# Sliding mixer of a hybrid layer: value products of both head sets joined, query tiles in turn, queries laid out by halves

## What is computed

```python
proj = rms_norm(h, norm_mix) @ w_in        # [qA|kA|vA|qB|kB|vB]
oa = sliding_window_sink_attention(qa, ka, va, sinks, bias_a)   # 8 heads of 64, 2 key heads
ob = differential_attention(qb, kb, vb, lam, ...)               # 4 heads, dense, causal by chunk
h = h + concat(oa, ob) @ w_out

# sliding window: chunks of 64 queries, each sees its own chunk and the one before
sc = einsum('bcqhgd,bckhd->bchgqk', qc, kb) * HEAD_DIM ** -0.5 + bias
probs = softmax(concat([sc, sink]))[..., :-1]
o = einsum('bchgqk,bckhd->bcqhgd', probs, vb)
```

## Time and profile before

| | before |
|---|---|
| median of 3 runs (lowest, highest) | 1290.88 us (1290.87, 1291.49) |
| the profiled execution: its time, its span | 1291.0 us, 1289.2 us |
| granted TensorE clock, mean | 0.987 |
| PE busy | 94% of the span |
| VectorE, ScalarE, GpSimd busy | 68%, 40%, 25% |

### The profile page before, as it was taken

The page is one execution under the profiler, slowest core; times in us unless marked ns, Lnnn a source line. Parts: engine busy times, 40 slices in busy tenths (PEclk is TensorE's granted clock), DMA queues, the critical chain, the costliest instruction groups (busy, mean ns, idle before and its releaser), DMA issues.

```text
span 1289.2 us, 16975 instructions
## 1 busy us (share of the span) xinstructions
PE 1217.1 (94%) x6103; PEld 996.7 (77%) x6103; DVE 876.3 (68%) x1466; ACT 519.7 (40%) x1042; POOL 325.1 (25%) x335
## 2 busy tenths in 40 slices
PE   4999999999686799999999999999999999999997
PEld 3997787787565687888888888888888768888885
DVE  3432776777776276877877777878678997863442
ACT  4321664665554133433333333333344334642321
POOL 0000000444454011333223233133126780000000
PEclk9999999999889899999999999999999999999999
DMA  6364233012912411333323333323397534620101
GB/s 202 77 99 87 50 83 83 30 42 74 264 51 49 148 49 66 90 99 109 96 82 123 101 103 99 99 89 116 138 321 272 164 104 137 196 81 25 41 33 49
DMA packets 128669, 136.08 MB, mean 106 GB/s; under 512 B 15570, under 2 KB 93130, under 8 KB 128522
## 3 DMA queue, kind: packets, MB, share of 16 engines
q1 hardware_dynamic: 128586, 135.00, 34.9%
HBM read 96.77 MB, written 37.22 MB: 104 GB/s over the span
## 4 chain that ended last, share of the span: by engine, by line
PE 57%; DVE 7%; issue 2%; DMA 1%; SPq 0%; ACT 0%; POOL 0%; POOLq 0%; DVEq 0%; ACTq 0%
PE ps L1680 56%; DVE wbuf L1180 4%; DVE more L1180 1%; DVE h L1606 1%; PE ps L1690 1%; DMA raw<-u_ops 1%; DMA raw<-in_w_out 1%; PE ps L1886 1%; SPq L479 0%; ACT wbuf L799 0%; DVE conv L1403 0%; PE ps L2040 0%; POOL stat L678 0%; DVE xs L1465 0%; DVE gel L1673 0%
## 5 line engine op out<-in xcount | busy, mean ns | idle before, releaser
L1680 PE MATMUL ps<-act_t,wbuf 128*128 128x512 f32 x1200 | 288.8, 396 | 2.9 <-DVE wbuf L1180 2.9
L1680 PEld LDWEIGHTS ps<-act_t,wbuf 128*128 128x128 f32 x1200 | 225.7, 188 | 57.5 <-issue 3.3
L1680 PE MATMUL ps<-wbuf 128*128 128x512 f32 x912 | 217.1, 392 | 2.1 <-DVE wbuf L1180 2.1
L1680 PEld LDWEIGHTS ps<-wbuf 128*128 128x128 f32 x912 | 170.1, 188 | 40.9 <-DVE wbuf L1180 4.1
L1680 PE MATMUL ps<-act_t,wq 128*128 128x512 f32 x624 | 155.7, 402 | 3.6 <-DVE wq L1182 2.8
L1680 PEld LDWEIGHTS ps<-act_t,wq 128*128 128x128 f32 x624 | 114.6, 188 | 33.4 <-issue 7.4
L1180 DVE TENSOR_TENSOR wbuf<-raw,wbuf 128x512 fp32r<-128x512 f32 (+1 forms) x107 | 105.1, 983 | 21.3 <-ACT wbuf L799 21.0
L678 POOL TENSOR_TENSOR stat<-stat 128x1 f32<-128x1 f32 x32 | 17.6, 551 | 360.6 <-DVE stat L1189 360.6
L799 ACT ACTIVATE wbuf<-raw 128x512 fp32r<-128x512 f32 (+1 forms) x107 | 69.3, 649 | 93.3 <-PE ps L1680 65.5
L1680 PE MATMUL ps<-hx,wbuf 128*128 128x512 f32 x408 | 96.2, 391 | 0.0
L1680 PEld LDWEIGHTS ps<-hx,wbuf 128*128 128x128 f32 x408 | 76.5, 188 | 16.6
(11 more groups left out here) (197 smaller groups left out, 2056.8 us busy)
## 6 DMA issues: line engine op xcount, KB each, us to landing
u_ops<-wbuf_f SPq DMA_DIRECT2D x77, 256.0 KB, 2.2
raw<-u_ops SPq DMA_DIRECT2D x77, 256.0 KB, 2.7
raw<-in_w_ffn_in SPq DMA_DIRECT2D x33, 512.0 KB, 3.9
g_ffn<-in_w_ffn_in SPq DMA_DIRECT2D x11, 512.0 KB, 4.1
act_f<-in_w_ffn_out SPq DMA_DIRECT2D x21, 256.0 KB, 3.8
w_raw<-in_w_in SPq DMA_DIRECT2D x10, 512.0 KB, 4.5
wbuf_f<-in_w_ffn_out SPq DMA_DIRECT2D x18, 256.0 KB, 6.9
x_in<-in_x SPq DMA_DIRECT2D x8, 512.0 KB, 3.7
```

What stands on the lines that cost most here:

```text
L1680: return nc.tensor.matmul(dst, lhs, rhs, start=start, stop=stop)
```

## The change

It does four things. (1) Items run in another order: n is the tile of queries n // 2 and the head set n % 2. (2) The value products of both sets of a tile are joined in 12 matmuls of 256 columns, in every even round from 4 on; the turned probabilities alternate between two halves of `a_t`, the loop has a round more, `a_ohi` and `a_olo` belong to item n-4, and `mst_a` moves to a part of `e_t`'s room, in two pieces. (3) The queries lie by halves of the tokens; eight units come ahead of the loop, with the second head set's first half among them (`UNITS` puts unit 8 before unit 7), 16 half units in the loop, in rounds 0 to 3 and 6 to 17. (4) Loads of weight tiles move by one: tiles 3 to 6 are asked for ahead of the stores, then tile 7 + n // 4 after the store of item n = 0, 4, 8, 12.

```diff
@@ buffers
-    mst_a = a_t[:, :, HALF:2 * HALF]
+    mst_a = e_r[:, :, :, 2 * P:HALF]
-    q_a = wq[:, 4 * D:12 * D].rearrange("p (s l c u q) -> p s l c u q", s=2, l=2, c=NCH, u=2)
+    q_a = wq[:, 4 * D:12 * D].rearrange("p (h s l c u q) -> p h s l c u q", h=2, s=2, l=2, c=NCH // 2,
+                                          u=2)
@@ schedule
-    FIRST_UNITS = 7
+    FIRST_UNITS = 8
+    UNITS = [0, 1, 2, 3, 4, 5, 6, 8, 7, 9] + list(range(10, NUNIT))
+    def a_cols(n):
+        return slice(HALF * (n % 2), HALF * (n % 2 + 1))
+    def a_src(n):
+        return ps[0:HD, 6:8, 2 * P * (n % 2):2 * P * (n % 2 + 1)]
     def a_fill(n):
-        return n if n < NA + 2 else None
+        if n < 4:
+            return n
+        return n - 2 if 6 <= n < NA + 2 else None
@@ sync
-        for j in range(3, 6):
+        for j in range(3, 7):
             load_w(j)
         for n in range(NA):
             sp.wait_ge(S.a_olo, n + 1)
-            sp.dma_start(mix_a[n], bits(mst_a[0:HD])).then_inc(S.a_stored, 16)
+            sp.dma_start(mix_a[n % 2 * NT + n // 2].rearrange("d l (g x) -> d l g x", g=2), bits(mst_a[0:HD])
+                         ).then_inc(S.a_stored, 16)
             if n % 4 == 0:
-                load_w(6 + n // 4)
-            if n == NA - 1:
-                load_w(10)
+                load_w(7 + n // 4)
@@ scalar
...
         def after_unit(u):
-            if u % 2 == 1 and next_w[0] < NTILE:
+            if (u == FIRST_UNITS or u % 2 == 1) and next_w[0] < NTILE:
                 split_w(next_w[0])
...
+            if n == 2:
+                act.wait_ge(S.a_stored, 16 * NA)
-        for n in range(NA + 3):
+        for n in range(NA + 4):
-            if n >= 3:
-                m = n - 3
-                act.wait_ge(S.a_pv, m + 1)
+            if n >= 4:
+                m = n - 4
+                act.wait_ge(S.a_pv, m // 2 + 1)
                 if m >= 1:
                     act.wait_ge(S.a_stored, 16 * m)
-                copy(mst_a[0:HD, 0, :], ps[0:HD, 6 + m % 2, :], S.a_ohi)
+                copy(mst_a[0:HD, 0], a_src(m), S.a_ohi)
             if 2 <= n <= NA + 1:
                 m = n - 2
                 act.wait_ge(S.a_turned, m + 1)
-                copy(a_t[:, 0, 0:HALF], ps[:, 5, :], S.a_thi)
+                if m >= 2:
+                    act.wait_ge(S.a_pv, m // 2)
+                copy(a_t[:, 0, a_cols(m)], ps[:, 5, :], S.a_thi)
@@ tensor
         pe.wait_ge(S.vlo, NT)
-        pe.wait_ge(S.unit_lo, 6)
+        pe.wait_ge(S.unit_lo, 8)
-            if n >= 3:
-                m = n - 3
-                pe.wait_ge(S.a_tlo, m + 1)
+            if n >= 4 and n % 2 == 0:
+                t = n // 2 - 2
+                pe.wait_ge(S.a_tlo, 2 * t + 2)
                 for g in range(2):
                     for c in range(2):
                         for z, (a, b) in enumerate(SPLIT3):
-                            ins = mm(a_out(m, g, c), v_a[kr, vt, a, HD * g:HD * g + HD],
-                                     a_t[kr, b, at:at + P], z == 0, z == 2)
+                            rhs = a_t[kr, b, :].rearrange("k (s x) -> k s x", s=2)[:, :, at:at + P]
+                            ins = mm(a_out(g, c), v_a[kr, vt, a, HD * g:HD * g + HD],
+                                     rhs.rearrange("k s (e q) -> k s e q", e=2), z == 0, z == 2)
```

More of the change, by code:

```diff
@@ L114, in build @@
     early.close()
+    by_type = ExitStack()
+    e_r = sb(by_type, "e_r", [P, 2, 2, SEQ], F32R)
+    by_type.close()
     e_t = sb(attn, "e_t", [P, 2, 2, SEQ])
@@ L303, in build @@
     HALVES = 2 * (NUNIT - FIRST_UNITS)
+    def a_cols(n):
+        return slice(HALF * (n % 2), HALF * (n % 2 + 1))
+    def a_src(n):
+        return ps[0:HD, 6:8, 2 * P * (n % 2):2 * P * (n % 2 + 1)]
     def a_fill(n):
-        return n if n < NA + 2 else None
+        if n < 4:
+            return n
+        return n - 2 if 6 <= n < NA + 2 else None
     def b_fill(n):
-        return NA + 2 + n if n < HALVES - NA - 2 else None
+        return NA + n if n < HALVES - NA else None
     def turned_with(n):
@@ L353, in first_key @@
     def first_key(n, c):
-        return HD if n % NT == 0 and c == 0 else 0
+        return HD if n // 2 == 0 and c == 0 else 0
     def tile_dst(j, half, part):
@@ L362, in tile_dst @@
         if st < 2:
-            return q_a[:, st, part, NCH // 2 * half:NCH // 2 * (half + 1), u, :]
+            return q_a[:, half, st, part, :, u, :]
         return qk[:, st % 2, u, part, sl]
@@ L503, in _ @@
             if n == 10:
-                sp.wait_ge(S.a_pv, NA)
+                sp.wait_ge(S.a_pv, NT)
                 sp.wait_ge(S.a_stored, 16 * NA)
@@ L812, in split_w @@
             if j >= 2:
-                act.wait_ge(S.unit_done, 2 * (j - 1))
+                act.wait_ge(S.unit_done, 9 if j == 5 else 2 * (j - 1))
             copy(w_sl[:, j % 2, 0], w_raw[:, :, :], S.w_hi)
@@ L848, in unit_hi @@
         def unit_hi(u):
-            j, half = u // 2, u % 2
+            j, half = UNITS[u] // 2, UNITS[u] % 2
             act.wait_ge(S.unit_done, u + 1)
@@ L858, in _ @@
             unit_hi(u)
-            if u % 2 == 1:
+            if u in (1, 3, 5):
                 split_w((u + 3) // 2)
@@ L943, in _ @@
                     act.wait_ge(S.b_pv, m)
-                if m == 4:
-                    act.wait_ge(S.a_stored, 16 * NA)
+                if m == 0:
+                    act.wait_ge(S.a_pv, NT)
                 copy(a_t[:, 0, 0:w], psf[:, 5 * HALF:5 * HALF + w], S.b_thi)
@@ L1325, in fill_lo @@
                 after_unit(FIRST_UNITS + part // 2)
-        for n in range(NA + 3):
+        for n in range(NA + 4):
             if n < NA:
-                s = n // NT
+                s = n % 2
                 o = 32 * (n % 2)
@@ L1349, in _ @@
                 nc.vector.tensor_tensor(dif, neg, sink[0], ALU.add).then_inc(S.a_logits, 1)
-            if n >= 3:
-                m = n - 3
+            if n >= 4:
+                m = n - 4
                 dve.wait_ge(S.a_ohi, m + 1)
-                low(mst_a[0:HD, 1, :], ps[0:HD, 6 + m % 2, :], mst_a[0:HD, 0, :], S.a_olo)
+                low(mst_a[0:HD, 1], a_src(m), mst_a[0:HD, 0], S.a_olo)
             if 2 <= n <= NA + 1:
@@ L1356, in _ @@
                 dve.wait_ge(S.a_thi, m + 1)
-                low(a_t[:, 1, 0:HALF], ps[:, 5, :], a_t[:, 0, 0:HALF], S.a_tlo)
+                low(a_t[:, 1, a_cols(m)], ps[:, 5, :], a_t[:, 0, a_cols(m)], S.a_tlo)
             if 1 <= n <= NA:
@@ L1750, in c_unit, with a_out @@
             ins.then_inc(S.c_done, 1)
-        def a_out(m, g, c):
-            return ps[0:HD, 6 + m % 2, 2 * P * g:2 * P * (g + 1)].rearrange("d (e c q) -> d e c q", e=2, c=2)[:, :, c, :]
+        def a_out(g, c):
+            return ps[0:HD, 6 + g, :].rearrange("d (s e c q) -> d s e c q", s=2, e=2, c=2)[:, :, :, c, :]
         for u in range(FIRST_UNITS):
@@ L1781, in _ @@
             if n < NA:
-                s, t = n // NT, n % NT
+                s, t = n % 2, n // 2
                 if n >= 2:
                     pe.wait_ge(S.a_logits, n - 1)
-                if t == 0 and s == 1:
+                if t == NT // 2 and s == 0:
                     pe.wait_ge(S.unit_lo, 10)
@@ L1793, in _ @@
                             ins = mm(ps[:, 1 + 2 * (n % 2) + g, P * c + k0:P * (c + 1)],
-                                     q_a[rows, s, a, ch, :, :].rearrange("p u q -> p (u q)"),
+                                     q_a[rows, ch // 8, s, a, ch % 8, :, :].rearrange("p u q -> p (u q)"),
                                      k_a[rows, b, (ch - 1) * CHUNK + k0:(ch + 1) * CHUNK], m == 0, m == 2)
                 ins.then_inc(S.a_scores, 1)
-            if n >= 3:
-                m = n - 3
-                pe.wait_ge(S.a_tlo, m + 1)
-                if m >= 2:
-                    pe.wait_ge(S.a_olo, m - 1)
-                if m == 0:
+            if n >= 4 and n % 2 == 0:
+                t = n // 2 - 2
+                pe.wait_ge(S.a_tlo, 2 * t + 2)
+                if t >= 1:
+                    pe.wait_ge(S.a_olo, 2 * t)
+                if t == 0:
                     pe.wait_ge(S.vshift, 32)
@@ L1806, in _ @@
                         at = P * (2 * g + c)
-                        if first_key(m, c):
+                        if first_key(2 * t, c):
                             kr, vt = slice(HD, P), NT
                         else:
-                            kr, vt = slice(0, P), (m % NT if c else NT + m % NT)
+                            kr, vt = slice(0, P), (t if c else NT + t)
                         for z, (a, b) in enumerate(SPLIT3):
-                            ins = mm(a_out(m, g, c), v_a[kr, vt, a, HD * g:HD * g + HD],
-                                     a_t[kr, b, at:at + P], z == 0, z == 2)
+                            rhs = a_t[kr, b, :].rearrange("k (s x) -> k s x", s=2)[:, :, at:at + P]
+                            ins = mm(a_out(g, c), v_a[kr, vt, a, HD * g:HD * g + HD],
```

(1 more changed line is left out.)

## The result

The changed kernel takes 1316.7 us (median; 1315.0 to 1318.5 over four runs) against 1291.1 before (median of four, with a fourth run beside the three of the table above): the ratio is 1.020, interval 1.018 to 1.022. Forecast were 1315 us and a slower kernel. The profiled execution took 1316.8 us with a span of 1315.0, 25.8 more than before.

What follows compares the result with a forecast made beforehand. PE was taken to set the pace, 4.95 us a round without a gap. Terms -0.8 - 0.3 + 0.9 + 5.0 + 5.5 + 5.7 + 6.2 - 1.1 + 3.0 = +24.1 us on 1291.0 gave about 1315 us, range 1297 to 1321.

Steps and rivals of the forecast that it cites:

- Part 4 (SyncE's order): SyncE's queue: loads waiting for splits delay stores; PE stands 5.5, 5.7 and 6.9 us (last +6.2) in rounds 11, 15, behind loop.
- the landing of a store behind a load: SyncE's queue: a store right behind a load was taken to land after 5.3 us, 3.0 + 2.3.
- Part 3 (missing cover): Rounds 4 and 5 without half units: PE waits 2.8 us at round 5's transposes, 2.2 at round 6's value products; +5.0 us.
- Part 2: A whole unit ahead of the loop: -0.3 us, but PE waits about 1.6 us for its low part, +0.9 us.
- Part 1: Joined value products: 12 matmuls of 256 columns cost 1.44 us, a gain of 0.10 a tile, 0.8 us in all.
- the bound of 107 ns a matmul: Joined value products: 256 columns at 2.4 GHz need 107 ns, 1.28 us a tile, a gain of 2.1 us.
- The clock: PE at half speed for 3 us after long stalls: +3.0 us taken, lower end 0, upper end 6.
- 1 us for each long one: Clock cost for each of three long stalls, as part of the slow stretch falls into idleness; +3.0 us together.
- The sum: Whole kernel: all gains, waits and clock add to +24.1 us on 1291.0, about 1315 us.
- Rival A: SyncE's queue: stores are not delayed by the loads; +6.9 us, about 1298 us; chance 0.13.
- Rival B: All stalls bring a slow clock, and stores behind loads land 0.3 us later; +28 us, 1319 us; chance 0.15.
- Rival C: Rounds 4 to 6 and 10 to 17: PE's own work still sets the pace, not slower; 1289.4 us; chance 0.10.

Runs made afterwards that it cites:

- e1_order: Changed kernel with the loads of weight tiles 8, 9 and 10 moved behind the stores of items 6, 10 and 14; 1301.6 us, ratio to before 1.0076.
- e2_before_blocked: Kernel before with only two loads moved: weight tile 8 behind the store of item 5, tile 9 behind item 9; 1302.8 us, ratio 1.0083.
- e6_thirds: e5_bank5 with two units laid over rounds 0 to 5 in thirds, not halves, and tile 7's load behind the store of item 2; 1299.7 us, ratio 1.0064.
- e5_bank5: e1_order with the eighth unit written to PSUM bank 5, not bank 1, and the wait for `S.vlo` put ahead of all eight units; 1304.1 us, ratio 1.0102.
- e3_spin: Changed kernel with 82 matmuls of unread result added at six places where PE stands idle, no wait removed; 1311.4 us, ratio 1.0152.
- e9_late_wait: e6_thirds plus a second staging buffer for odd items, with ScalarE's wait for their stores two items later in the next loop; 1293.9 us, ratio 1.0019.

## Why the prediction was right

The time was forecast within 1.7 us, but by two errors that cancel. Point by point:

- **Part 4 (SyncE's order)** named mechanism, rounds and queue rightly; e1_order removes it, e2_before_blocked makes it in the other kernel. Its sizes were too large: 5.5, 5.7 and 6.9 us forecast, 4.37, 4.26 and 5.91 measured. The term that failed is the landing of a store behind a load, taken as 5.3 us and measured as 4.5, 4.4 and 4.3; the load's issue, too, takes 0.42 us and not 0.6. Together they make 1.0 to 1.2 us, where the waits were 1.1, 1.4 and 1.0 us shorter than forecast.
- **Part 3 (missing cover)**: 2.8 and 2.2 us forecast, 2.42 and 1.71 measured. With the cover spread, e6_thirds has no wait at the transposes of round 5 and 0.32 us at the value products of round 6, which confirms the cause.
- **Part 2**: the wait of 1.6 us was 1.50. Whether removing it helps is open: e5_bank5 exchanged it for one of 1.91 us ahead of the units.
- **Part 1**: 1.44 us for a joined group forecast, 1.48 measured. The interpolation over columns was closer than the bound of 107 ns a matmul; what is left of the gain is 0.5 us, not 0.8.
- **The clock** was mis-sized the other way: +3.0 forecast, with 6 as the upper end. Summed by the starts of the groups behind each wait, against the same groups at full clock, the changed kernel lost about 1.5 + 2.1 + 1.5 + 2.2 + 1.4 = 8.7 us. Two steps failed. The smaller one is "1 us for each long one, as part of the slow stretch falls into idleness": behind the three long waits none of it did, and they cost 1.5, 2.2 and 1.4, 5.1 us in place of 3.0. The larger one is that the shorter waits were put at nothing (only the upper end counted the pair): the 1.50 us ahead of the first scores cost 1.5 in this execution and the pair in rounds 5 and 6 cost 2.1, together 3.6. The earlier trace rows could have warned of it. The clock there was already low ahead of the 3 us of idleness, behind a wait of 1.61 us, in the kernel before:

```profile
325.94 0.44 PE L1842 MATMUL ps<-ident,bias_a 128*128 128x128 f32 x1 [1.61 <-POOL bias_a L703]
```
```profile
326.00:330.00 4.00, 3.94 (x23) 3.54 (x23) 1.77 (x6) 3.36 (x9) 1.42 (x4) 0.58 0.75 187
```

The Trainium skill's rule that idle gaps make the clock fall again, each time anew (TensorE: Matmul & The Clock Gate, "HAM oscillation — how this bites in real kernels") was the better guide for this kernel: clocks of 0.94, 0.66, 0.86, 0.76 and 0.72 stand in the stretches of the five waits. It does not hold for each gap of the later runs, as the last section shows. e3_spin gives 5.4 to 6.3 us of the 8.7 back.
- **The sum**: waits forecast 23.1 us (5.0 + 5.5 + 5.7 + 6.9), measured 18.7; clock forecast 3.0, measured 8.7. Less by 4.4 and more by 5.7: that the time came out within 1.7 us is luck in the sizes, though not in the causes. The loop took 102.0 us (132.44 to 234.46) where 105 were forecast.
- **Rival A** (1298 without SyncE's blocking) is what e1_order built, 1301.6. It had no clock in its sum: the slow groups of e1_order lost some 2.5 us in rounds 5 and 6, part of which fell into the wait before the value products, and 1.4 behind the loop. **Rival B** said the clock goes further, and it did, beyond B's 6 us, but the waits were shorter and not longer. **Rival C** fails, as PE stood 4.26 to 5.91 us at each of the three delayed stores.

## What to carry to other kernels

A queue that issues in order has a schedule of its own: when loads are renumbered in it, check for each the round in which its wait is met against the round in which it is reached, and what stands behind it. A load one place too early cost some 5 us each time, in a loop that moved no more data. Where a product engine sets the pace, price short idle gaps too, with the slow stretch that may follow (1.4 to 2.2 us here where it came), and spread the cover over the rounds before taking it from two of them. When a wait has to move for the sake of one step, put it before that step alone, and look in the trace at what it costs there: e5_bank5 lost by its new wait what it had gained.

## What had not been expected of the hardware

After a wait of only 1.50 us ahead of the first scores the clock fell in the changed kernel (12 matmuls from 133.26 to 137.80, 4.54 us), and did not in e1_order after the same wait (133.62 to 136.63, 3.01 us): the same idle time cost 0 or 1.5 us. Behind the loop it was the same: after 3.24 us of idleness the half unit took 4.33 us to the next start in e1_order (230.88 to 235.21) and 2.89 in e6_thirds (227.90 to 230.79). The 1.91 us ahead of the units cost nothing in e9_late_wait (clock 1.00 from 86 to 125 us). What an idle gap costs in clock is not settled by its length alone; what else decides was not tried. And matmuls of 128 columns whose weights have 64 columns are hardly slower per column than those of 256: 24 of them take 1.50 us, 62 ns each, and 12 of the others 1.48, 123 ns each.
